# The 1/rms of a token moves from ahead of the turn to the copy behind the first projection

## The reference

```python
def rms_norm(x, g):
    xf = x.astype(jnp.float32)
    y = xf * lax.rsqrt(jnp.mean(xf * xf, axis=-1, keepdims=True) + NORM_EPS_2)
    return (y * g.astype(jnp.float32)).astype(x.dtype)

for l in range(DEPTH):
    h = rms_norm(x, g_attn[l])
    z = h @ w_in[l]
    c_q, c_kv, k_pe, z_dil, z_dsa, z_qi, z_ki, z_wi = jnp.split(z, offsets, axis=-1)
    ...                      # three kinds of attention from the parts of z, joined to mix
    x = x + mix @ w_o[l]
    h = rms_norm(x, g_ffn[l])
    u = causal_dwconv(h @ w_up[l], conv_w[l], conv_b[l])
    gate, up = u[..., :D_FF], u[..., D_FF:]
    x = x + (jax.nn.silu(gate) * up) @ w_down[l]
return rms_norm(x, g_final)
```

## Time and profile before

| | us |
|---|---|
| median of 3 timed runs | 2332.2 |
| lowest and highest | 2329.93, 2336.22 |
| the profiled execution's own time | 2321.24 |
| its span, first to last instruction | 2319.4 |
| PE busy in the span | 2066.6 (89%) |
| DVE busy | 736.9 (32%) |
| ACT busy | 354.8 (15%) |
| head of the first attention layer: block's first PE work to first projection matmul | 1456.60 to 1467.48 |
| the same in the second layer | 1879.48 to 1890.37 |

### The profile page before, as it was taken

How to read it: one execution, slowest core, us unless ns; L and a number is a source line. 1 busy time by engine, 2 the same in 40 slices (tenths; PEclk the granted TensorE clock), 3 DMA queues, 4 the chain that set the end, 5 groups by cost and what they waited for, 6 DMA issues and landing times. The chain is left out here.

```text
span 2319.4 us, 32708 instructions
## 1 busy us (share of the span) xinstructions
PE 2066.6 (89%) x13473; PEld 1381.3 (60%) x13473; DVE 736.9 (32%) x2203; ACT 354.8 (15%) x947; POOL 93.0 (4%) x94
## 2 busy tenths in 40 slices
PE   8999999888888796999888887798899989789997
PEld 7677576556556344666655564344688444448863
DVE  4455332222222208322222223276222015722211
ACT  2122111000000104100000001114121001412100
POOL 0112000000000200000000000000002000000110
PEclk9999979888888995877988888898899989889998
DMA  9422469999999841479999999540344344124420
GB/s 329 145 109 109 184 238 385 425 426 426 427 426 426 319 148 36 182 309 421 426 427 427 426 426 411 196 145 4 133 164 149 123 145 145 37 73 145 149 87 27
DMA packets 111998, 564.53 MB, mean 243 GB/s; under 512 B 12392, under 2 KB 15646, under 8 KB 79134
## 3 DMA queue, kind: packets, MB, share of 16 engines
q1 hardware_dynamic: 111902, 563.20, 61.1%
HBM read 562.13 MB, written 1.05 MB: 243 GB/s over the span
## 5 line engine op out<-in xcount | busy, mean ns | idle before, releaser
L655 PE MATMUL ps<-ring,arena 128*32 128x256 f32 x3968 | 272.7, 435 | 80.1 <-issue 56.1
L2333 PE MATMUL ps<-arena,ring 128*128 128x256 f32 x1408 | 308.1, 382 | 1.6 <-DVE arena L249 1.6
L2333 PEld LDWEIGHTS ps<-arena,ring 128*128 128x128 f32 x1408 | 270.0, 192 | 39.7 <-DVE arena L249 2.4
L655 PEld LDWEIGHTS ps<-ring,arena 128*32 128x32 f32 x3968 | 160.3, 125 | 194.4 <-issue 146.9
L636 PEld LDWEIGHTS ps<-arena 128*128 128x128 f32 x2048 | 241.9, 197 | 25.5 <-issue 25.5
L1598 PE MATMUL ps<-ring,arena 128*128 128x512 f32 (+1 forms) x576 | 248.9, 592 | 3.3 <-PEq L1113 1.7
L636 PE MATMUL ps<-arena 128*128 128x32 f32 x2048 | 248.9, 282 | 0.0
L271 PE MATMUL ps<-ring,arena 128*128 128x512 f32 x480 | 206.9, 593 | 0.8 <-ACT arena L2205 0.8
L694 PE MATMUL ps<-ring,arena 128*32 128x256 f32 x1984 | 177.9, 520 | 26.8 <-issue 25.9
L1598 PEld LDWEIGHTS ps<-ring,arena 128*128 128x128 f32 x576 | 109.3, 191 | 135.9 <-issue 133.3
L271 PEld LDWEIGHTS ps<-ring,arena 128*128 128x128 f32 x480 | 91.0, 190 | 114.2 <-issue 112.9
(11 more groups left out here) (299 smaller groups left out, 1807.6 us busy)
## 6 DMA issues: line engine op xcount, KB each, us to landing
ring<-in_moe_w_gate_dram SPq DMA_DIRECT2D x62, 2048.0 KB, 19.1
ring<-in_moe_w_up_dram SPq DMA_DIRECT2D x62, 2048.0 KB, 23.6
ring<-in_moe_w_down_dram SPq DMA_DIRECT2D x62, 2048.0 KB, 20.9
ring<-in_w_up_dram SPq DMA_DIRECT2D x22, 2048.0 KB, 7.9
ring<-in_ssm_w_in_dram SPq DMA_DIRECT2D x12, 2048.0 KB, 10.2
ring<-in_w_in_dram SPq DMA_DIRECT2D x10, 2048.0 KB, 13.7
ring<-in_w_down_dram SPq DMA_DIRECT2D x10, 2048.0 KB, 7.7
ring<-in_attn_w_qkv_dram SPq DMA_DIRECT2D x6, 2048.0 KB, 20.9
```

The source lines that it names most:

```text
L655: mm = nc.tensor.matmul(ps[j * CAP:(j + 1) * CAP, 5, 0:256], xg[:, b, k * CAP:(k + 1) * CAP], w[:, k, (j % 2) * 256:(j % 2 + 1) * 256], st ...
L2333: mm = nc.tensor.matmul(ps[:, n % 4, 0:SEQ], w[:, k, k4 * P:(k4 + 1) * P], xT_mlp[:, k, :], start=(k == 0), stop=(k == KD - 1))
```

## The change

In the two attention layers the tokens are turned as they stand in `h`. DVE evicts the turned banks with the gain, as before, and only then works out 1/rms; a memset behind the chain signals `scaled`. ACT waits for `scaled` ahead of its first copy, and each of the twelve copies multiplies its rows with the token's 1/rms (`row_scale`). The tile `tn` is gone. The MLP layers and the last normalisation are as they were.

```diff
-        def act_project(act, chunks, dst, cols, lo, hi, bank):
+        def act_project(act, chunks, dst, cols, lo, hi, bank, row_scale=None):
...
-                nc.scalar.activation(dst[:, tt, cols[q]:cols[q] + n_cols], ps[:, bank + n % 4, 0:n_cols], ACT.Copy)\
+                nc.scalar.activation(dst[:, tt, cols[q]:cols[q] + n_cols], ps[:, bank + n % 4, 0:n_cols], ACT.Copy,
+                                     scale=1.0 if row_scale is None else row_scale[:, tt:tt + 1])\
                     .then_inc(projected_copied.sem, 1)
...
-        tn = area(8080, TT, D)
...
-        def dve_scale(dve, dst):
-
+        def dve_row_scale(dve):
             dve.wait_ge(squared.sem, squared.at(1))
             V(nc.vector.tensor_scalar(rms_v[:, 0:2], rms_s[:, 0:2], 1.0 / D, EPS2, ALU.mult, ALU.add))
             rsqrt(rms_r[:, 0:2], rms_v[:, 0:2], rms_t[:, 0:2])
+
+        def dve_scale(dve, dst):
+            dve_row_scale(dve)
             for tt in range(TT):
...
-                    pe.wait_ge(scaled.sem, scaled.at(1))
-                    pe_turn(pe, tn)
+                    pe_turn(pe, h)
                     pe.wait_ge(turned_copied.sem, turned_copied.at(4))
...
-                    act_project(act, c_in2[l], zz, cols, 0, 4, 4)
+                    act.wait_ge(scaled.sem, scaled.at(1))
+                    act_project(act, c_in2[l], zz, cols, 0, 4, 4, rms_r)
...
-                    act_project(act, c_in2[l], zz, cols, 4, 10, 4)
+                    act_project(act, c_in2[l], zz, cols, 4, 10, 4, rms_r)
...
-                    act_project(act, c_in2[l], zz, cols, 10, 12, 4)
+                    act_project(act, c_in2[l], zz, cols, 10, 12, 4, rms_r)
...
-                    dve_scale(dve, tn)
                     dve.wait_ge(params2_turned.sem, params2_turned.at(1))
                     V(nc.vector.tensor_copy(pcol[:, 0:195], ps[:, 4, 0:195]))
                     dve_turn_scaled(dve, xT_att, g_att)
+                    dve_row_scale(dve)
+                    nc.vector.memset(rms_t, 0.0).then_inc(scaled.sem, 1)
```

## The result

The changed kernel took 2313.79 us (median of 4, 2307.95 to 2317.04) against 2332.45 us for the kernel before (4 runs, 2329.93 to 2336.22). The ratio is 0.9914, with a 95% interval of 0.9895 to 0.9932: faster by 16 to 24 us, where 13.0 were forecast. The profiled execution has a span of 2315.2 us, only 4.2 under the one of before; it started its first attention head 4.2 us later, at 1460.76 instead of 1456.60, behind blocks that the change doesn't touch. So the two profiled executions tell where time went, not how much was gained.

The account below looks back on a forecast made before the run. PE, busy 89% of the span, was taken as the bound, waiting on DVE at both attention heads. First layer -6.0 + 1.4, second -6.1 - 0.7 - 1.8, copies +0.2: -13.0, from 2332.2 to 2319.2 us; range 2313 to 2326.

Parts of the forecast that it names:

- 3.9 were forecast: First attention layer: slack in us between the signal of `scaled` and ACT's first copy, its reader; so cost 0.
- the first layer's clock: First attention head: PE's turn and projection start at half clock; charged +1.4 us, a mean of four starts, bounds 0 and 1.9.
- Rival B: Both attention heads are lucky with the clock, no loss in the first layer: -14.4 us, 2317.8; chance 0.08.
- The start of the turn: Both attention heads: token transposes follow the parameter transposes without waiting, 6.0 us earlier in the first layer, 6.1 in the second.
- The second layer: Second attention head: if the clock stays full, the turn gains 0.7 us and the projection's start 1.8.
- rival A: Second attention head: the clock falls anyway, so -0.7 and -1.8 are lost: -10.5 us, 2321.7; chance 0.30.
- The two scaled writes: DVE in each attention head: they leave the path, 1.42 us together; the first of them was said to let PE turn.
- The copies: ACT's twelve scaled copies per layer: 83 ns more each, all but the last hidden, +0.2 us, between 0 and 0.4.
- Rival C: Attention stage: the shift makes more unit pairs run at the slow clock; chance 0.13 mild, 0.03 full (2337.8 us).
- its mild form: Attention stage: 6 more of 16 pairs run slow, +7.4 us, 2326.6; chance 0.13, shared with a gain drowned in scatter.
- this sign: Attention layers: prediction wrong if the head's gain is there but the distance from projection's end to output sum has grown.

## Why the prediction was right or wrong

**The mechanism was right, and the direction.** Both heads lost their wait, `scaled` came 6.4 and 4.2 us ahead of its reader (3.9 were forecast), no other wait took its place, no transfer got in the way.

**The size was wrong, in two steps.** The lower edge of the range was 2313; the first measurement's ratio puts the time at 0.9914 x 2332.2 = 2312.1, a gain of 20 us where 13.0 were forecast (the median itself, 2313.79, is not below the edge). The first step that failed is a term of the sum, the +1.4 us charged for the first layer's clock: against the median it measures +0.2 (next but one paragraph), so the forecast time was 1.2 us too long by it. Rival B had the charge taken out, at 2317.8, and the range started from there, so the charge alone did not put the result outside. The second is the last of the numbers, "I add 3 to 4 us on either side": executions of one kernel scatter with a deviation of 2.9 to 3.5 us, and a median of four against a median of four can lie 4 us off for that alone. Most of the miss is this scatter: the gain over all executions, 15.1 us, give or take 1.8, puts the changed kernel at 2317 on the scale of the prediction, inside the range and 2 us from the forecast.

**The start of the turn**, -6.0 and -6.1: seven traces after show 6.07 and 6.21 us less from the block's first PE work to the turn. Right.

**The first layer's clock**, +1.4: this is the term that was set against the wrong thing. It was right against the profiled execution, whose fast start was luck; in seven of seven traces the changed kernel starts slow there and loses 42.1 - 39.97 = 2.1 us. But the kernel before lost 1.9 us there in all three further traces, so against them the term is 42.08 - 41.90, +0.2. The prediction saw that three of four starts are slow, and even that this execution "had luck there", and then took the difference over to the median without taking the charge out: "the head is the same work in them" holds for the work and not for its clock. The four starts that it averaged are of one execution, so they could show that starts differ, not that executions do; that is shown by 39.97 against 41.75 to 42.12 us.

**The second layer**, -0.7 and -1.8 if the clock stays: it stayed in three of seven traces and fell in four, which is rival A, given 0.30, where the text took the other as likelier. Over the seven the terms are 10.87 - 3.73 = 7.1 us for the head (6.2 to the turn's start and 0.9 from there to the projection, where 6.1 and 0.7 were forecast). The evictions take 2.48 us for four, not four times 0.735, so it is 3.45 us from the block's first PE work where the clock stays and 3.9 to 4.0 where it falls. For the projection's start it is 0.75 (1.8 were forecast). Two errors of opposite sign: the pacing too dear, the clock too hopeful.

**The two scaled writes**: the text said that the first of them lets PE turn; it is the second. The sum was not touched, since it went by the turn's start.

**The copies**, +0.2: 91 ns each and 3.04 instead of 2.95 us ahead of the last transposes, 0.09 us a layer. Right.

**Rival C**, the clock in the attention stage: it is in the traces of the first layer, far below the 7.4 us of its mild form. From the projection's start to the sum with w_o it takes 145.0 us after (seven traces) and 144.0 before (the three further ones), and in two of the seven the sum with w_o took 30.18 and 30.22 us, with a slow start, instead of 27.73. By its own last sentence the prediction is wrong "if the gain in the head is there and the distance from the projection's end to the output sum has grown": it has, from 51.4 to 52.3 us on average in the first layer (51.3 and 51.5 in the second), so this sign came up, at 0.8 us. In the execution profiled first it was 49.3. Whether the shift causes it is not shown: four of the seven have the 51.3 to 51.7 of before, the other three 52.8 to 53.5. The projection of the MLP in the same layer is 0.8 us shorter.

**The sum** of the measured terms is -6.1 + 0.2 - 7.1 - 0.75 + 0.2 = -13.6 us. That the spans of the traces differ by 13.5 us is not the same sum: the rest of them happens to cancel. Blocks ahead of the first head are 0.4 us shorter, the units of the first layer 0.75 longer and those of the second 0.1, the first sum with w_o 0.7 longer, the two MLP projections 0.8 and 0.3 shorter. The forecast of 13.0 is near 13.6 because its errors cancelled: the forecast time was too long by 1.2 us for the first layer's clock, by 0.3 for the second head and by 0.1 for the first, and too short by 1.05 for the second projection's start. That is luck. One reading of the chances does not add up either: 0.46 + 0.30 + 0.08 is 0.84, so 0.85 holds 0.01 of C's 0.13 and not half of it.

## What to carry to other kernels

Where PE waits, price the wait and the clock behind it, and read the clock's share from several executions: here one start took 39.97 us in one trace and 41.75 to 42.12 in three others. A term that corrects for luck in the profiled execution must not be carried over to the median. Linear work that only scales rows can go behind the product, into a copy that is made anyway, if its result comes before the first product does.

## What the runs showed of the hardware

PE needs no useful work to keep its clock or get it back: 24 and 44 transposes of an identity in the kernel's rest brought 7.0 us without one shorter wait. The 24 ran at half clock (5.33 us), and the turn behind them at full clock (1.97 us instead of 3.68). Nor does work alone hold it: in four of seven executions it fell some 0.9 us after the second head's first PE work, with the turn under way, behind a rest of 1.9 us. And a turn at full clock makes DVE's evictions back to back, 2.48 us for four of 128x512 (0.60 each from start to start, the last 0.69), where a turn at half clock spaces them to 3.2 us. The first attention head's place is set by SP in all but one of the 17 traces: its last load before the barrier took 5.3 to 6.6 us to issue, and PE's first work came 0.44 or 0.45 us behind its end. In the changed kernel that was 1460.31 and 1460.76, with the DMA engines busy throughout (387 GB/s):

```profile
1454.46 5.85 SPq L114 DMA_DIRECT2D ring<-in_w_in_dram  x1
```

In the exception, the first of the three further executions of before, POOL's addition to `h` ended last, 0.51 us before PE's first work.
